# Splitting weights into high and low halves once per load of 1024 columns instead of twice per load of 512

## What is computed

```python
xn = rmsnorm(x, norm_gain)
rq, rk, rv, rg, sq, sk, sv, sg, gr, gs = split(xn @ w_in)      # w_in is 2048 x 14336
o_ret = retention(rope(rq), rope(rk), rv)                       # 8 heads, d_k 128, d_v 256
o_sb  = stick_breaking(sq, sk, sv, cached k and v)              # 8 heads, d 128
ret_branch = groupnorm(o_ret) * gain * silu(rg)                 # 2048 wide
sb_branch  = o_sb * silu(sg)                                    # 1024 wide
merged = sigmoid(gr) * (ret_branch @ w_ret_proj) + sigmoid(gs) * (sb_branch @ w_sb_proj)
y = rmsnorm(x + merged @ w_out) * final_norm_gain
```

## Time and profile before

| | us |
|---|---|
| median of 3 runs | 2322.53 |
| lowest and highest run | 2321.79, 2322.84 |
| span of the profiled execution | 2320.0 |
| PE busy in it | 2270.7 (98%) |
| DVE busy | 1070.8 (46%) |
| ACT busy | 650.8 (28%) |
| POOL busy | 109.2 (5%) |
| granted TensorE clock, all but the first and last of 40 slices | 0.9 or more of full speed |

### The profile page before, as it was taken

One profiled execution on the slowest core, in us unless ns is written; L12 is line 12 of the kernel. 1 busy time (PEld: TensorE's weight loads), 2 busy tenths in 40 slices (PEclk: granted clock), 3 DMA queues, 4 the chain that ended last, 5 costly groups with the idle time before them and its releaser, 6 DMA issues.

```text
span 2320.0 us, 44559 instructions
## 1 busy us (share of the span) xinstructions
PE 2270.7 (98%) x17064; PEld 2183.6 (94%) x17064; DVE 1070.8 (46%) x1481; ACT 650.8 (28%) x1166; POOL 109.2 (5%) x161
## 2 busy tenths in 40 slices
PE   5999999999999999999999999999999999999996
PEld 4999999999999999999999999999999999999996
DVE  4333444334555543365554655556555443332223
ACT  5333433334422221222222122222222222222223
POOL 4001111011100000000000000000000000000000
PEclk8999999999999999999999999999999999999998
DMA  5444444444333355323323323232243344434333
GB/s 149 134 119 126 133 136 122 116 127 128 102 98 109 109 178 167 89 81 94 102 82 98 97 80 100 88 102 88 82 121 96 114 131 129 132 110 114 106 97 129
DMA packets 450235, 262.04 MB, mean 113 GB/s; under 512 B 22530, under 2 KB 436354, under 8 KB 448898
## 3 DMA queue, kind: packets, MB, share of 16 engines
q1 hardware_dynamic: 450178, 261.27, 38.1%
HBM read 228.17 MB, written 33.03 MB: 113 GB/s over the span
## 4 chain that ended last, share of the span: by engine, by line
PE 97%; POOL 1%; ACT 1%; DVE 0%; DMA 0%; ACTq 0%; DVEq 0%; issue 0%; SPq 0%; POOLq 0%
PE ACC L558 84%; PE Z L578 3%; PE Z L628 1%; PE Z L824 1%; PE Z L825 1%; PE Z L816 1%; PE Z L704 1%; POOL XL L1643 1%; PE Z L642 1%; PE Z L610 1%; PE Z L678 1%; PE Z L789 1%; PE Z L801 1%; PE Z L803 0%; DMA XN<-in_x_prompt 0%; ACTq L1205 0%
## 5 line engine op out<-in xcount | busy, mean ns | idle before, releaser
L558 PE MATMUL ACC<-XH,HI 128*128 128x288 f32 x4096 | 895.3, 300 | 6.4 <-POOL XL L1643 6.4
L558 PE MATMUL ACC<-XH,LO 128*128 128x288 f32 x4096 | 877.9, 296 | 0.0
L558 PE MATMUL ACC<-XL,HI 128*128 128x288 f32 x4096 | 876.0, 295 | 0.0
L1224 DVE TENSOR_TENSOR LO<-RAW,HI 128x512 fp32r<-128x512 f32 x608 | 425.0, 700 | 657.7 <-ACT HI L931 612.0
L931 ACT ACTIVATE HI<-RAW 128x512 fp32r<-128x512 f32 x608 | 382.2, 630 | 1072.6 <-PE ACC L558 858.3
L558 PEld LDWEIGHTS ACC<-XH,HI 128*128 128x128 f32 x4096 | 656.8, 189 | 26.4 <-issue 15.0
L558 PEld LDWEIGHTS ACC<-XH,LO 128*128 128x128 f32 x4096 | 659.4, 189 | 0.0
L558 PEld LDWEIGHTS ACC<-XL,HI 128*128 128x128 f32 x4096 | 659.3, 189 | 0.0
L558 PE MATMUL ACC<-RL,HI 128*128 128x288 f32 x768 | 164.5, 296 | 0.0
L558 PE MATMUL ACC<-RH,HI 128*128 128x288 f32 x768 | 164.5, 296 | 0.0
L558 PE MATMUL ACC<-RH,LO 128*128 128x288 f32 x768 | 164.4, 296 | 0.0
(11 more groups left out here) (172 smaller groups left out, 1429.0 us busy)
## 6 DMA issues: line engine op xcount, KB each, us to landing
RAW<-in_w_in SPq DMA_DIRECT2D x224, 512.0 KB, 3.9
KC<-in_cache_sb_k SPq DMA_DIRECT2D x256, 64.0 KB, 1.9
VC<-in_cache_sb_v SPq DMA_DIRECT2D x256, 64.0 KB, 2.4
RAW<-in_w_ret_proj SPq DMA_DIRECT2D x32, 512.0 KB, 4.1
RAW<-in_w_out SPq DMA_DIRECT2D x32, 512.0 KB, 3.9
RAW<-in_w_sb_proj SPq DMA_DIRECT2D x16, 512.0 KB, 4.4
ST<-in_state_ret SPq DMA_DIRECT2D x64, 128.0 KB, 2.6
out<-ST SPq DMA_DIRECT2D x64, 128.0 KB, 1.8
```

The lines of the kernel that those rows point to most:

```text
L558: mm = pe.matmul(ACC[a][:, half, 0:HALF], w[:, s, k, :], x[:, k0 + k, half * HALF:(half + 1) * HALF], start=first and k == 0 and w is HI a ...
L1224: dve.tensor_tensor(LO[:, s], RAW[:, r, (n % 2) * QK:(n % 2 + 1) * QK, :], HI[:, s].bitcast(F32), ALU.subtract).then_inc(S[f"w_full{s}"], 1)
```

## The change

HI and LO hold the same bytes, but as 2 slots of 1024 columns instead of 4 of 512. ACT and DVE split only at every second call of `split()`, a whole load at a time. Calls 0 and 2 stand in the prologue, and from then on the calls that split are those of the odd bodies. A slot is taken by PE in the first quarter of a load (`w_full`) and freed by its second (`w_free`). RAW and the loads are as before.

```diff
-_W = {... ("hi_full", 1, 4), ("w_full", 1, 4), ("w_free", 1, 4)) ...}
+_W = {... ("hi_full", 1, 2), ("w_full", 1, 2), ("w_free", 1, 2)) ...}
...
-        HI, _ = sb("HI", [P, 4, QK, P], F32R)
-        LO, _ = sb("LO", [P, 4, QK, P], F32R)
+        HI, _ = sb("HI", [P, 2, 2 * QK, P], F32R)
+        LO, _ = sb("LO", [P, 2, 2 * QK, P], F32R)
...
# PE, quarter()
-                s, a = slot[0] % 4, group[0] % 2
+                s, kb, a = slot[0] // 2 % 2, slot[0] % 2 * QK, group[0] % 2
...
-                t.take(f"w_full{s}")
+                if kb == 0:
+                    t.take(f"w_full{s}")
...
-                            mm = pe.matmul(ACC[a][:, half, 0:HALF], w[:, s, k, :],
+                            mm = pe.matmul(ACC[a][:, half, 0:HALF], w[:, s, kb + k, :],
...
-                else:
+                elif kb:
                     mm.then_inc(S[f"w_free{s}"], 1)
...
# ACT, split()
-                s, r = n % 4, n // 2 % 2
-                if n % 2 == 0:
-                    t.take(f"raw_in{r}", 16)
+                s = n // 2 % 2
+                if n % 2:
+                    return
+                t.take(f"raw_in{s}", 16)
                 t.room(f"w_free{s}")
-                act.activation(HI[:, s], RAW[:, r, (n % 2) * QK:(n % 2 + 1) * QK, :], ACT.Copy)\
-                    .then_inc(S[f"hi_full{s}"], 1)
+                act.activation(HI[:, s], RAW[:, s], ACT.Copy).then_inc(S[f"hi_full{s}"], 1)
...
# DVE, split()
-                s, r = n % 4, n // 2 % 2
+                s = n // 2 % 2
+                if n % 2:
+                    return
                 t.take(f"hi_full{s}")
-                dve.tensor_tensor(LO[:, s], RAW[:, r, (n % 2) * QK:(n % 2 + 1) * QK, :], HI[:, s].bitcast(F32),
-                                  ALU.subtract).then_inc(S[f"w_full{s}"], 1)
-                if n % 2:
-                    dve.drain().then_inc(S[f"raw_free{r}"], 1)
+                dve.tensor_tensor(LO[:, s], RAW[:, s], HI[:, s].bitcast(F32), ALU.subtract)\
+                    .then_inc(S[f"w_full{s}"], 1)
+                dve.drain().then_inc(S[f"raw_free{s}"], 1)
```

More of the change, by code:

```diff
@@ L50 @@
 T_DP, T_DS, T_KP, T_KS, T_GC, T_G8, T_QP, T_QS, T_KC, T_W = 0, 128, 192, 193, 201, 202, 203, 331, 339, 340
-_W = {f"{n}{s}": k for n, k, r in (("raw_in", 16, 2), ("raw_free", 1, 2), ("hi_full", 1, 4), ("w_full", 1, 4),
-                                   ("w_free", 1, 4)) for s in range(r)}
+_W = {f"{n}{s}": k for n, k, r in (("raw_in", 16, 2), ("raw_free", 1, 2), ("hi_full", 1, 2), ("w_full", 1, 2),
+                                   ("w_free", 1, 2)) for s in range(r)}
 def per(loads, act0=0, act1=0, dve0=0, dve1=0, **more):
```

## The result

The changed kernel takes 2333.01 us (median of 4 runs, 2330.9 to 2333.49), the kernel before 2322.16 us in the same comparison: a ratio of 1.0045, 95% interval 1.0031 to 1.0059. It is slower by 10.8 us where 8.1 were forecast.

A forecast was written before the change was run, and what follows sets the result against it. PE's matmuls were taken as the bound, busy 2270.7 of 2320.0 us. Five terms summed to 8.05 us; with 2.5 us from span to median this gave 2330.6 us, range 2325.5 to 2335.

The forecast's parts named there:

- saved time worth nothing: Splits on ACT and DVE: 61 and 52 us saved beside PE, counted as 0 in the sum.
- (1): w_sb's fifth quarter: later gate, load, longer split and MO make PE start late, +2.75 us.
- (2): w_ret's fifth quarter: the late gate delays load and split, without MO, +1.5 us.
- (3): Last head's attention beside the gates: PE's wait for LL from POOL grows, +0.9 us.
- (4): OV in each of 8 heads: copied behind the longer split, 0.33 us a head, +2.6 us.
- eight waits: Sign in the profile after: eight waits of PE L578 for OV, 0.3 us each.
- (5): Prologue: two longer subtractions alternating with POOL's XL move the first matmul, +0.3 us (-0.3 to +0.8).
- PE's stream is the same: PE throughout: the same 24 matmuls to a quarter, one wait fewer in two quarters, 0 us.
- Thin covers: KTT and other small reserves are used up by longer splits; 2333 to 2336 us, chance 0.14.
- Only the stage changes: OV and the last head keep their times; about 2327.1 us, chance 0.16.
- The covers: Reserves hold everywhere, stage changes included, leaving only crumbs; 2322.5 to 2325 us, chance 0.14.
- faster: DVE and ACT finish sooner, so PE's waits for them shrink; 2320.5 us, chance 0.04.

The follow-up runs named there:

- all late steps put right: Changed kernel, large splits kept, with OV's copy, the loads, body 7's attention and gate, and the prologue's XT and XH reordered around splits or stores: 2320.3 us.
- the load ahead: Changed kernel with SP issuing the load for the fifth and sixth quarters of w_sb and w_ret before the last gate's store: 2327.36 us.
- the two halves: Changed kernel with each split made as two copies and two subtractions of 512 columns, each half signalled by itself: 2326.31 us.
- extra products at w_sb: Changed kernel with 20 unused products on PE in its wait right before w_sb's fifth quarter: 2331.57 us.
- OV ahead: Changed kernel with DVE copying OV before the subtraction of 1024 columns in body 11 of each stick-breaking head: 2329.58 us.
- LL alone: Changed kernel with only LL's chain beside the gates moved: body 7's attention and gate before the split, DVE's split behind body 8's attention: 2330.05 us.
- small splits with the altered prologue: Kernel before, splits of 512, with one split before the prologue's last XT and XH, two behind, and 26 unused products on PE: 2319.31 us.

## Why the prediction was right, point by point

**The bound, and saved time worth nothing.** Right: 39.5 and 64 us less on DVE and ACT show nowhere in PE's time. With all late steps put right, large and small splits are 0.3 us apart.

**The number.** The sum of the steps was 3.2 us too low (8.05 for the 11.3 between the spans), the time only 2.4 (2330.6 for 2333.0). The 0.8 between them is luck: the 2.5 us from span to median were taken over from before, and after the change they were 1.7. And 2333.01 lies at the very end of the bracket of 2328.5 to 2333 that held the forecast's own chance.

**(1) Gates to w_sb.** The chain was right link by link: gate late, load behind it, 4.5 us until the copy, split, MO. The step measured is 2.9 us and 0.3 in the second matmul; forecast 2.75. Two sizes were short: measured against PE the load went 2.0 us later, not 1.85, and the 0.15 us between the subtraction and MO took 0.38. What came behind the wait was left out, see below. That the load was the cause is shown by the run with the load ahead.

**(2) Gates to w_ret.** 1.7 for 1.5, by the same chain, and gone with the load ahead.

**(3) LL.** 0.8 for 0.9; that the split ahead of body 7's attention was the cause is shown by the run that moves it.

**(4) OV.** 2.7 for 2.6, shown by removing it, and a second time by the two halves. It was called the thinnest term; it held since both durations did, within 7 ns. The sign that the prediction named for it, eight waits of PE, did not appear as such; the steps in the starts show it.

**(5) Prologue.** 0.9 for 0.3, outside the -0.3 to +0.8 given. Two subtractions took 4.52 us, near the upper end of 3.6 to 4.7:

```profile
36.67 4.52 DVE L1227 TENSOR_TENSOR LO<-RAW,HI 128x1024 fp32r<-128x1024 f32 x2 [1.65 <-ACT HI L933]
```

They take 2.46 us alone; the 2.06 more are about two turns of POOL at the prediction's 1.1 us. The middle of the range was taken where the row of three subtractions, each with its turn of POOL, spoke for the upper end.

**The term that was missing.** "PE's stream is the same ... 0 too" was wrong. The matmuls are the same, but twelve at w_sb and some eleven in the prologue ran at the lower clock that had run at the higher one before, 1.2 us each time. That is 2.4 of the 3.5 us between the sum of 8.05 and 11.6. The rest is 0.6 in the prologue and 0.5 at w_sb. A new wait of PE was priced at its length alone. How much of the 2.4 us a median holds isn't known: the part in the prologue came and went between runs with the same prologue (0 to 1.2 us), and the part at w_sb stayed away in one of the three other profiles with that wait left empty.

**The rivals.** Thin covers did not break: KTT shows no step. The upper durations that it needed didn't come; the measured time lies near its 2334, but by the clock, not by its mechanism. (Half-way from 8.05 to 14.4 is 11.2, not the 11.5 written there.) "Only the stage changes" falls with the steps at OV and LL. The covers did not hold, and nothing was faster.

## What to carry to other kernels

When a buffer's slots become fewer and larger, write down for each engine which instruction now stands behind the wait for the slot, and who wants its result: the engine time saved is worth nothing where the engine isn't the bound, and an order that was harmless becomes the cost. What repaired all of it here is order: move the wanted step ahead of the split, and the load ahead of the store it doesn't depend on (12.7 us). Halves behind the same late wait repaired about half (6.7 us). Price a new wait of TensorE at its length or more: 0 to 3 us more in these profiles.

## What the runs showed of the hardware

- Waits of PE of 2.8 to 2.9 us were followed by a granted clock of 0.50 in three profiles and not in one; filled with extra products, in one profile, it stayed up. Waits of 1.8 us did it in some (3.0 us lost behind LL in two profiles, 1.5 in a third, 1.5 behind w_ret in one) and not in others (behind LL in the changed kernel and in the run with the extra products at w_sb). What decides it between two executions of the same length of wait these runs don't show.
- The rise after the prologue came 3.3 us after the first matmul of the projection in the kernel before and 5.9 us after it in the changed one. In four runs with the changed kernel's prologue it came 4.2, 4.4, 3.5 and 3.3 us after it, so the change alone doesn't set it.
- Kernels with such waits spread wider in some cases: 7.1 us over 5 runs (OV ahead) and 4.9 over 6 (LL alone), against 0.9 over 11 with all late steps put right. But the two halves, with waits of 2.1 and 1.4 us, spread 1.1 over 11, and the kernel with all late steps put right and the extra products, which has no such wait, 2.2 over 11, so the waits aren't shown to be the cause.
- At the full clock matmuls of 288 columns followed each other at 0.133 us in the first head of most profiles, but at 0.130 up to 72 us in two (small splits with the altered prologue; LL alone). It was worth 0.6 us; no run shows why.
